# First modulation groups made as columns, and K and Q split earlier, in a diffusion backbone kernel on one core

## Chip, core and metric

The kernel runs as one program on 1 core of a Trainium2 chip. The metric is the device time of one execution in microseconds (us); lower is better. TensorE is written PE below, VectorE DVE, ScalarE ACT, and the queue that issues most of the loads SP.

## What is computed

Two layers of a backbone over 256 latent and 256 context tokens of width 1024, all in f32. Each layer is a gated feed-forward half step, a token mixer (retention with 4 heads beside a short convolution), and a second half step. Every sub-layer starts with a modulated norm. Cut to what the change touches:

```
def adaln_params(cond, w_mod, b_mod):
    m = jax.nn.silu(cond) @ w_mod + b_mod
    return m.reshape(cond.shape[0], 1, N_MOD, D_MODEL)

def modulated_norm(h, w, mod, i):
    return rmsnorm(h, w) * (1.0 + mod[:, :, 3 * i + 1]) + mod[:, :, 3 * i]

def swiglu(y, w_up, w_down):
    a, b = jnp.split(y @ w_up, 2, axis=-1)
    return (jax.nn.silu(a) * b) @ w_down
...
    scores = jnp.einsum('bhnid,bhnjd->bhnij', qf, kf) * intra_decay[None, :, None]
    intra = jnp.einsum('bhnij,bhnje->bhnie', scores, vf)
```

`modulated_norm` of the first sub-layer needs shift and scale (sections 0 and 1 of `w_mod` of layer 0, 2048 columns) before the first product with `w_up` can start. The retention needs K and Q (rotated by the rope), and decay matrices that are sums of masked exponentials.

## The kernel before, in words

Every engine runs an order written out by hand; semaphores join them. A product with a weight is made in single precision out of three fast ones: each weight block of 128x1024 is loaded to `RAW`, ACT copies it to a rounded `HI` (L1066), DVE makes the rest `LO` (L1514), and PE multiplies HI and LO with the high and low half of the activations `Y`. A unit is such a block with its products. There are 6 weight slots, and a load waits until the unit that had the slot before is done.

**The beginning** (stage "ada"). PE turns the rows of x and ctx (L852), ACT and DVE copy them to `H` (`h_copy`). SP loads `w_mod` in 16 blocks `WM` of 512 KB, with the blocks of the first four units between them: WM 0, 1, unit 0, WM 2, 3, unit 1, WM 4, 5, unit 2, WM 6, 7, unit 3, WM 8 to 15. Four blocks make one of four groups `g`; blocks 4g and 4g+1 give its scale (`sec` 1), 4g+2 and 4g+3 its shift (`sec` 0). `modulation(b)` multiplies block b, with the two conditions SiLU(c), SiLU(c_ctx) stationary in 32-column strips `SCW` and 256 columns of the block moving (L812, four strips of the array at once). ACT copies the sums to `ADAROWS` (`rows_out`, L1201), and `columns(g, sec)` turns them to columns on PE (L822). DVE adds the bias (`mods0`, L1737), ACT makes the high half of y (`y0`, L1209), DVE the low half (`y0_full`, `y0_low`, L1753 and L1760). `first_units(ks, units)` is what PE makes of y: for the k-blocks `ks` it adds into the banks of the units (L836, L840). Group g gives y for k = 2g and 2g+1. `keep_clock(n)` are n idle products of ones (L779), which fill stretches of PE. An f32 product that isn't the fast kind is shown by the trace as two records on PE.

**Stage "v"**. PE makes V in 8 steps `cc` (L931). Beside it DVE ropes K and Q in steps 0 to 3; in steps 2 to 5 ACT makes the four exponentials of one head (L1359), which wait for DVE's sums `DEC` of the head before (L1956), and then `KQH`, the rounded copy of two heads of K or Q (L1365). DVE in steps 3 to 6 masks and sums the exponentials (L1953, L1956, L1959) and then makes `KQL`, the rest of K or Q (L1964). Stage "ret" waits on PE for all four `KQL`, then makes the scores (L942 to L944) of heads 0 and 1; DVE multiplies them with `DEC` into `PX` and `PC` (`probs`, L1978), and `outputs(0)` on PE (L970) waits for those.

Of the kernel before, what the change touches and what calls it, by code (L numbers as in the profile page):

```python
# [7 lines left out]
F32 = mybir.dt.float32  # L8
F32R = mybir.dt.float32r
ACT = mybir.ActivationFunctionType  # L10
# [118 lines left out]
def plan():  # L129
# [70 lines left out]
    for at, s in enumerate(p.stages):  # L200
        after = p.stages[at + 1] if at + 1 < len(p.stages) else None
        if s.kind == "ada":
            s.turn = [p.acc(b) for b in (7, 5, 6, 4, 0, 1, 2, 3)]
            s.vec_acc = p.acc(6)
            s.rb_acc = p.acc(6)
            s.rows = [[p.acc(4), p.acc(5)] for g in range(4)]
            s.cols_acc = [[p.acc(6), p.acc(7)] for g in range(4)]
            after.halves = []
        elif s.kind in ("up", "k"):
# [99 lines left out]
def build(nc, x, c, ctx_in, c_ctx, norm_w, w_mod, b_mod, up1, down1, w_in, log_decay, conv_w,  # L309
# [76 lines left out]
    with es:  # L386
# [99 lines left out]
        def drain_wait(eng, acc):  # L486

            eng.wait_ge(drained[acc.bank], acc.use)
# [17 lines left out]
        def follows(s):  # L506
            return stages[stages.index(s) + 1]
# [110 lines left out]
        def _(pe):  # L618
# [180 lines left out]
            for s in stages:  # L799
                T = s.T  # L800
                if s.kind == "ada":
                    up_s = follows(s)

                    def modulation(b):

                        g, sec = b // 4, 1 - b % 4 // 2
                        acc = s.rows[g][sec]
                        if b % 2 == 0:
                            bank_wait(pe, acc)
                        pe.wait_ge(wm_landed[b], 16)  # L810
                        for kk in range(4):
                            ins = mm(B[acc.bank][32 * kk:32 * kk + 32, 0:GROUP], SCW[:, 4 * (b % 2) + kk, :],  # L812
                                     WM[b][:, kk, :], start=(b % 2 == 0), stop=(b % 2 == 1),
                                     tile_position=(0, 32 * kk))
                        ins.then_inc(wm_used, 1)
# [45 lines left out]
                                            ).then_inc(vec_turned, 1)  # L861
                    pe.wait_ge(sc_wide, 1)
                    modulation(0)
                    drain_wait(pe, s.turn[0])
                    keep_clock(3, s.turn[0].bank)
                    modulation(1)
                    bank_wait(pe, s.rb_acc)
                    pe.wait_ge(diag_done, 4)
                    mm(B[6][:], ONES[:], DIAG[:], start=True, stop=True).then_inc(rb0_done, 1)
                    columns(0, 1)  # L870
                    drain_wait(pe, s.turn[6])
                    keep_clock(5, s.turn[6].bank)
                    modulation(2)
                    keep_clock(3, s.turn[6].bank)
                    modulation(3)
                    keep_clock(2, s.turn[6].bank)
                    columns(0, 0)
                    drain_wait(pe, s.turn[7])
                    keep_clock(5, s.turn[7].bank)
                    first_units((0, 1), (0,))  # L880
                    modulation(4)
                    modulation(5)
                    first_units((0, 1), (1,))
                    columns(1, 1)
                    first_units((0, 1), (2,))
                    modulation(6)
                    modulation(7)
                    columns(1, 0)
                    first_units((0, 1), (3,))
                    first_units((2,), range(4))  # L890
                    first_units((3,), (0, 1))
                    for b in range(8, 12):
                        modulation(b)
# [162 lines left out]
        def _(act):  # L1056
# [136 lines left out]
            for s in stages:  # L1193
                T, cols = s.T, s.cols
                if s.kind == "ada":
                    def rows_out(g, sec):
                        acc = s.rows[g][sec]
                        act.wait_ge(wm_used, 4 * g + 4 - 2 * sec)
                        if g >= 2:
                            act.wait_ge(cols_done, 2 * (g - 1) - sec)  # L1200
                        A(ADAROWS[:, g % 2, sec, :], B[acc.bank][:, 0:GROUP], ACT.Copy).then_inc(drained[acc.bank], 1)  # L1201

                    def y0(*ks):
# [13 lines left out]
                    act.wait_ge(x_summed, 3)  # L1217
                    act.wait_ge(ctx_summed, 1)
                    A(RT4[:], SS4[:], ACT.Sqrt, bias=EPST[:, 0:1], scale=1.0 / D).then_inc(x_rooted, 1)
                    h_copy(0, 1, 3)  # L1220
                    rows_out(0, 1)
                    h_copy(6)
                    split_upto(0)
                    rows_out(0, 0)
                    y0(0, 1)
                    split_upto(2)
                    rows_out(1, 1)
                    split_upto(3)
                    rows_out(1, 0)
                    y0(2, 3)  # L1230
                    rows_out(2, 1)
                    rows_out(2, 0)
                    y0(4)
# [110 lines left out]
                elif s.kind == "v":  # L1344
# [3 lines left out]
                    for cc in range(8):  # L1348
                        step(s.u + cc)
                        if cc == 0:  # L1350
                            swapped(s.layer, 1, QTT, stages[stages.index(s) - 1].acc)
                        if 2 <= cc < 6:

                            h = cc - 2
                            f, b = LG[:, lgw + h:lgw + h + 1], LG[:, lgw + HEADS + h:lgw + HEADS + h + 1]
                            for n, (col, g) in enumerate(((CM_RELP, f), (CM_RELN, b), (CM_CF, f), (CM_CB, b))):
                                if h or s.layer:
                                    act.wait_ge(dec_done, 2 * (HEADS * s.layer + h) - (1 if n < 2 else 0))
                                A(G4[:, n, :], CM[:, col:col + 512], ACT.Exp, scale=g).then_inc(exp_done, 1)  # L1359
                        if 2 <= cc < 6:  # L1360

                            g = cc - 2
                            heads, n = slice(2 * (g % 2), 2 * (g % 2) + 2), 512 if g < 2 else follows(s).T
                            act.wait_ge(rope_done, 4 * s.layer + g + 1)
                            A(KQH[:, heads, g // 2, 0:n], (KTT, QTT)[g // 2][:, heads, 0:n], ACT.Copy).then_inc(kq_hi, 1)  # L1365
                        if cc % 4 == 3:
                            act.wait_ge(unit_done, s.u + cc + 1)
                            for tt in range(4):
                                b = s.acc[4 * (cc // 4) + tt].bank
                                A(V[:, tt, (cc // 4) * 512:(cc // 4 + 1) * 512], B[b][:], ACT.Copy  # L1370
                                  ).then_inc(drained[b], 1)
# [132 lines left out]
        def _(dve):  # L1504
# [221 lines left out]
            for s in stages:  # L1726
                T, cols = s.T, s.cols
                if s.kind == "ada":
# [68 lines left out]
                    split_upto(2)  # L1797
                    xn(2, 3)
                    mods0(1, 1)
                    split_upto(3)  # L1800
                    mods0(1, 0)
                    y0_full(2)
                    y0_low(2)
                    y0_full(3)
                    y0_low(3)
                    xn(4, 5, 6, 7)
# [112 lines left out]
                elif s.kind == "v":  # L1919
# [5 lines left out]
                    for cc in range(8):  # L1925
                        step(s.u + cc)
                        if cc < 4:
# [16 lines left out]
                                             ).then_inc(rope_part, 1)  # L1944
                            dve.wait_ge(rope_part, 2 * n + 2)
                            V_.tensor_tensor(src, a, b, ALU.add).then_inc(rope_done, 1)
                        if 3 <= cc < 7:

                            h = cc - 3
                            e, dp = 4 * (HEADS * s.layer + h), 2 * (HEADS * s.layer + h)  # L1950
                            for n, (g, op) in enumerate(((0, ALU.is_ge), (1, ALU.is_le))):
# [6 lines left out]
                            dve.wait_ge(exp_done, e + 4)  # L1958
                            V_.tensor_tensor(DEC[:, h, 2:4, :].rearrange("p a n -> p (a n)"), G4[:, 2, :], G4[:, 3, :],  # L1959
                                             ALU.add).then_inc(dec_done, 1)  # L1960
                            g = cc - 3
                            heads, n = slice(2 * (g % 2), 2 * (g % 2) + 2), 512 if g < 2 else follows(s).T
                            dve.wait_ge(kq_hi, 4 * s.layer + g + 1)
                            V_.tensor_tensor(KQL[g // 2][:, heads, 0:n], (KTT, QTT)[g // 2][:, heads, 0:n],  # L1964
                                             KQH[:, heads, g // 2, 0:n].bitcast(F32), ALU.subtract).then_inc(kq_lo, 1)
                elif s.kind == "ret":
                    nP, nO = s.nP, s.nO
                    dve.wait_ge(dec_done, 2 * HEADS * (s.layer + 1))
# [190 lines left out]
```

## Time and profile before

| | |
|---|---|
| median of 3 runs | 2143.64 us (2143.31 to 2145.12) |
| profiled execution, its own time | 2144.41 us |
| its span, first to last instruction | 2142.5 us |
| PE busy | 2128.9 us, 99% |
| DVE busy | 1410.8 us, 66% |
| ACT busy | 785.3 us, 37% |
| mean granted clock of PE | 0.999 |
| mean rate of loads | 148 GB/s |

The span is what instructions cover; the 1.9 us beyond it lie around it. Busy time of PE counts records that overlap in its pipeline, so that the start-to-start distance of records tells what one costs, not its length.

### The profile page before, as it was taken

The numbers are of one execution on the slowest core, as the hardware profiler recorded it, in microseconds if no ns is written. First come the engines' busy times: TensorE is split into PE (matmuls) and PEld (weight loads), VectorE is DVE, ScalarE is ACT, GpSimd is POOL, SyncE is SP. The second block draws the span as 40 slices with busy tenths as digits, with TensorE's granted clock in tenths as the row PEclk, the third lists the DMA queues.
The fourth block names the chain that finished last, engine by engine and source line by source line (L and its number), as shares of the span: only waits on it lengthen the run. The fifth ranks groups of instructions, "written<-read, shape, count | busy, mean of one in ns | idle before, by whom it ended". The sixth has DMA issues, their size and how long they took to land.

```text
span 2142.5 us, 26254 instructions
## 1 busy us (share of the span) xinstructions
PE 2128.9 (99%) x10667; PEld 1803.6 (84%) x10667; DVE 1410.8 (66%) x1929; ACT 785.3 (37%) x1158; POOL 0.2 (0%) x4
## 2 busy tenths in 40 slices
PE   9999999999999999999999999999999999999998
PEld 6888888988888888898888888888889888888887
DVE  5677777657588873477777767733335678777765
ACT  4322222444322222342222234222223555556654
POOL 0000000000000000000000000000000000000000
PEclk9999999999999999999999999999999999999999
DMA  8655555341455553345555544433333537775664
GB/s 261 196 168 176 158 166 163 123 117 38 123 164 157 177 157 94 94 139 166 175 165 163 163 141 141 135 98 99 91 99 106 157 90 200 205 213 139 187 189 145
DMA packets 454395, 318.13 MB, mean 148 GB/s; under 512 B 10478, under 2 KB 429702, under 8 KB 453894
## 3 DMA queue, kind: packets, MB, share of 16 engines
q1 hardware_dynamic: 432476, 243.43, 39.4%
q10 hardware_dynamic: 21800, 73.03, 10.0%
q8 instruction: 85, 1.39, 0.3%
q14 instruction: 34, 0.28, 0.0%
HBM read 312.23 MB, written 1.05 MB: 146 GB/s over the span
## 4 chain that ended last, share of the span: by engine, by line
PE 96%; DVE 1%; ACT 1%; SPq 1%; DMA 0%; issue 0%; DVEq 0%
PE bank L628 23%; PE bank L630 23%; PE bank L629 23%; PE bank L626 9%; PE bank L627 5%; PE bank L659 2%; PE bank L931 2%; PE bank L970 1%; PE bank L693 1%; PE bank L694 1%; PE bank L695 1%; PE bank L663 1%; SPq L551 1%; PE bank L836 1%; PE bank L769 0%; ACT G L1359 0%
## 5 line engine op out<-in xcount | busy, mean ns | idle before, releaser
L1514 DVE TENSOR_TENSOR LO<-RAW,HI 128x1024 fp32r<-128x1024 f32 (+1 forms) x435 | 522.9, 1206 | 344.9 <-ACT HI L1066 344.7
L628 PE MATMUL bank<-Y,HI 128*128 128x512 f32 (+1 forms) x1440 | 555.7, 386 | 0.0
L630 PE MATMUL bank<-Y,LO 128*128 128x512 f32 (+1 forms) x1440 | 553.6, 384 | 0.0
L629 PE MATMUL bank<-Y,HI 128*128 128x512 f32 (+1 forms) x1440 | 553.5, 384 | 0.0
L1066 ACT ACTIVATE HI<-RAW 128x1024 fp32r<-128x1024 f32 (+1 forms) x435 | 441.6, 1039 | 118.0 <-DVE MODACC L1525 36.3
L628 PEld LDWEIGHTS bank<-Y,HI 128*128 128x128 f32 x1440 | 270.6, 188 | 54.2 <-issue 1.3
L630 PEld LDWEIGHTS bank<-Y,LO 128*128 128x128 f32 x1440 | 270.6, 188 | 54.0
L629 PEld LDWEIGHTS bank<-Y,HI 128*128 128x128 f32 x1440 | 270.7, 188 | 53.4 <-issue 0.5
L1525 DVE SCALAR_TENSOR_TENSOR MODACC<-MODRAW,SC,MODACC 128x1024 f32<-128x1024 f32 x224 | 277.2, 1279 | 3.7 <-DMA MODRAW<-in_w_mod_dram 3.3
L626 PE MATMUL bank<-Y,HI 128*128 128x512 f32 x720 | 253.8, 397 | 0.0
L628 PE MATMUL bank<-Z,HI 128*128 128x512 f32 (+1 forms) x594 | 218.0, 367 | 0.0
L630 PE MATMUL bank<-Z,LO 128*128 128x512 f32 (+1 forms) x594 | 217.1, 366 | 0.0
L629 PE MATMUL bank<-Z,HI 128*128 128x512 f32 (+1 forms) x594 | 217.1, 365 | 0.0
L1257 ACT ACTIVATE TMP<-bank 128x512 f32<-128x512 f32 x66 | 39.5, 598 | 455.9 <-PE bank L630 372.2
L627 PE MATMUL bank<-Y,LO 128*128 128x256 f32 x720 | 201.1, 279 | 0.0
L626 PEld LDWEIGHTS bank<-Y,HI 128*128 128x128 f32 x720 | 135.2, 188 | 32.3
L627 PEld LDWEIGHTS bank<-Y,LO 128*128 128x128 f32 x720 | 135.7, 188 | 0.1
L628 PEld LDWEIGHTS bank<-Z,HI 128*128 128x128 f32 x594 | 112.0, 189 | 18.2
L629 PEld LDWEIGHTS bank<-Z,HI 128*128 128x128 f32 x594 | 112.1, 189 | 18.1
L630 PEld LDWEIGHTS bank<-Z,LO 128*128 128x128 f32 x594 | 112.0, 189 | 17.8
L1634 DVE SCALAR_TENSOR_TENSOR H<-bank,GATE,H 128x256 f32<-128x256 f32 x64 | 28.3, 479 | 122.1 <-PE bank L630 122.1
L1836 DVE TENSOR_TENSOR TMP<-bank,TMP 128x512 f32<-128x512 f32 x66 | 45.5, 690 | 74.7 <-PE bank L630 74.7
(276 smaller groups left out, 2422.8 us busy)
## 6 DMA issues: line engine op xcount, KB each, us to landing
RAW<-in_ffn_w_up_dram SPq DMA_DIRECT2D x174, 512.0 KB, 3.9
MODRAW<-in_w_mod_dram ACTq DMA_DIRECT2D x128, 512.0 KB, 4.4
RAW<-in_w_in_dram SPq DMA_DIRECT2D x128, 512.0 KB, 4.1
RAW<-in_ffn_w_down_dram SPq DMA_DIRECT2D x66, 512.0 KB, 4.0
RAW<-in_ffn_w_down_dram SPq DMA_DIRECT2D x24, 384.0 KB, 3.5
WM<-in_w_mod_dram SPq DMA_DIRECT2D x16, 512.0 KB, 8.9
RAW<-in_w_ret_out_dram SPq DMA_DIRECT2D x16, 512.0 KB, 4.8
RAW<-in_w_conv_out_dram SPq DMA_DIRECT2D x16, 512.0 KB, 4.5
```

Of the source, the lines that this page charges most:

```text
L626: mm(bank[:].rearrange("p (a n) -> p a n", a=2), hi, X[:, k, :, cols], start=first, stop=False)
L627: return mm(bank[:, 0:HALF], lo, X[:, k, 0, cols], start=False, stop=end)
L628: mm(bank, hi, X[:, k, 0, cols], start=first, stop=False)
L629: mm(bank, hi, X[:, k, 1, cols], start=False, stop=False)
L630: return mm(bank, lo, X[:, k, 0, cols], start=False, stop=end)
L659: mm(B[cc][:, cols], wblock(s.u + cc, part, k), Y[:, k, 0, cols], start=(k == 0 and part == 0), stop=False)
L931: ins = mm(B[s.acc[4 * half + tt].bank][:], Y[:, k, a, tt * P:(tt + 1) * P], w[u % SLOTS][:, kk * 512:(kk + 1) * 512], start=(k == 0 and ( ...
L1066: A(weights(v, 0), raw_weights(v), ACT.Copy).then_inc(hi_done, 1)
L1257: A(TMP[:, o % 2, cols], B[s.acc[cc].bank][:, cols], ACT.Silu).then_inc(drained[s.acc[cc].bank], 1)
L1514: V_.tensor_tensor(weights(v, 1), raw_weights(v), weights(v, 0).bitcast(F32), ALU.subtract).then_inc(lo_done, 1)
L1525: V_.scalar_tensor_tensor(acc, MODRAW[i % 2][:], a, acc, ALU.mult, ALU.add).then_inc(mod_step, 1)
L1836: V_.tensor_tensor(TMP[:, 2 + o % 2, cols], B[s.acc[cc].bank][:, cols], TMP[:, o % 2, cols], ALU.mult).then_inc(drained[s.acc[cc].bank], 1)
```

## The change

Groups 0 and 1 of the modulation (blocks 0 to 7) are multiplied the other way round: the block is stationary, 128 columns at a time, and the two conditions move, so that the sums come out as columns. `rows_out` and `columns` of these groups go. The order of PE's beginning is rewritten, with other counts for `keep_clock`; the fourth unit (unit 3) joins at k = 2 instead of before it, and `HI` and `LO` of unit 3 come later on ACT and DVE. In stage "v" `KQH` is made one step earlier and ahead of the exponentials, and `KQL` one step earlier and ahead of the masks.

```
             s.rb_acc = p.acc(6)
-            s.rows = [[p.acc(4), p.acc(5)] for g in range(4)]
+            s.rows = [[p.acc(4), p.acc(5)] if g >= 2 else None for g in range(4)]
...
                         g, sec = b // 4, 1 - b % 4 // 2
+                        if g < 2:
+                            acc = s.cols_acc[g][sec]
+                            if b % 2 == 0:
+                                bank_wait(pe, acc)
+                            pe.wait_ge(wm_landed[b], 16)
+                            for kk in range(4):
+                                for m in range(2):
+                                    ins = mm(B[acc.bank][:, 2 * m:2 * m + 2], WM[b][:, kk, m * P:(m + 1) * P],
+                                             SC[:, :, 4 * (b % 2) + kk], start=(b % 2 == 0 and kk + m == 0),
+                                             stop=(b % 2 == 1 and kk == 3 and m == 1))
+                            if b % 2 == 1:
+                                ins.then_inc(cols_done, 1)
+                            return
...
                     modulation(0)
-                    drain_wait(pe, s.turn[0])
-                    keep_clock(3, s.turn[0].bank)
-                    modulation(1)
                     bank_wait(pe, s.rb_acc)
                     pe.wait_ge(diag_done, 4)
                     mm(B[6][:], ONES[:], DIAG[:], start=True, stop=True).then_inc(rb0_done, 1)
-                    columns(0, 1)
+                    modulation(1)
+                    drain_wait(pe, s.turn[1])
+                    keep_clock(8, s.turn[1].bank)
+                    modulation(2)
+                    keep_clock(5, s.turn[1].bank)
+                    modulation(3)
                     drain_wait(pe, s.turn[6])
-                    keep_clock(5, s.turn[6].bank)
-                    modulation(2)
-                    keep_clock(3, s.turn[6].bank)
-                    modulation(3)
-                    keep_clock(2, s.turn[6].bank)
-                    columns(0, 0)
                     drain_wait(pe, s.turn[7])
-                    keep_clock(5, s.turn[7].bank)
+                    keep_clock(7, s.turn[1].bank)
                     first_units((0, 1), (0,))
                     modulation(4)
                     modulation(5)
                     first_units((0, 1), (1,))
-                    columns(1, 1)
                     first_units((0, 1), (2,))
                     modulation(6)
                     modulation(7)
-                    columns(1, 0)
-                    first_units((0, 1), (3,))
-                    first_units((2,), range(4))
+                    keep_clock(6, s.turn[7].bank)
+                    first_units((2,), range(3))
+                    first_units((0, 1, 2), (3,))
                     first_units((3,), (0, 1))
...
-                    h_copy(0, 1, 3)
-                    rows_out(0, 1)
-                    h_copy(6)
+                    h_copy(0, 1, 3, 6)
                     split_upto(0)
-                    rows_out(0, 0)
                     y0(0, 1)
                     split_upto(2)
-                    rows_out(1, 1)
+                    y0(2)
                     split_upto(3)
-                    rows_out(1, 0)
-                    y0(2, 3)
+                    y0(3)
...
                     mods0(1, 1)
-                    split_upto(3)
                     mods0(1, 0)
                     y0_full(2)
                     y0_low(2)
+                    split_upto(3)
```

PE, the beginning, from the first modulation to the first unit. Before (`SCW` the conditions, `WM_72` to `WM_75` blocks 0 to 3, `x4` instructions in a row):

```order
L812 MATMUL bank<-WM_72,SCW 32x256 x4
L779 MATMUL bank<-ONES 128x128 x3
L812 MATMUL bank<-WM_73,SCW 32x256 x4
L869 MATMUL bank<-DIAG,ONES 128x512
L822 MATMUL bank<-CK,ADAROWS 128x2 x2
L779 MATMUL bank<-ONES 128x128 x5
L812 MATMUL bank<-WM_74,SCW 32x256 x4
L779 MATMUL bank<-ONES 128x128 x3
L812 MATMUL bank<-WM_75,SCW 32x256 x4
L779 MATMUL bank<-ONES 128x128 x2
L822 MATMUL bank<-CK,ADAROWS 128x2 x2
L779 MATMUL bank<-ONES 128x128 x5
```

And of the changed kernel, the same place on PE:

```order
L814 MATMUL bank<-SC,WM_72 128x2 x8
L879 MATMUL bank<-DIAG,ONES 128x512
L814 MATMUL bank<-SC,WM_73 128x2 x8
L779 MATMUL bank<-ONES 128x128 x8
L814 MATMUL bank<-SC,WM_74 128x2 x8
L779 MATMUL bank<-ONES 128x128 x5
L814 MATMUL bank<-SC,WM_75 128x2 x8
L779 MATMUL bank<-ONES 128x128 x7
```

A modulation is now 8 instructions of the form that `columns` had (128 stationary columns, 2 moving) in place of 4, and 20 idle products stand where 18 did, with the two `columns` gone.

PE further on, where unit 3 (`HI_112`, `LO_106`) joins. Before, from blocks 6 and 7:

```order
L812 MATMUL bank<-WM_78,SCW 32x256 x4
L812 MATMUL bank<-WM_79,SCW 32x256 x4
L822 MATMUL bank<-CK,ADAROWS 128x2 x2
L836 MATMUL bank<-Y,HI_112 128x512
L836 MATMUL bank<-Y,LO_106 128x512
L840 MATMUL bank<-Y,HI_112 128x512
```

And of the changed kernel:

```order
L814 MATMUL bank<-SC,WM_78 128x2 x8
L814 MATMUL bank<-SC,WM_79 128x2 x8
L779 MATMUL bank<-ONES 128x128 x6
L849 MATMUL bank<-Y,HI_109 128x512
L849 MATMUL bank<-Y,LO_103 128x512
L849 MATMUL bank<-Y,HI_110 128x512
```

Units 0 to 2 take k = 2 first, and unit 3 stands behind them with its nine products.

DVE in stage "v" of layer 0, the last head (`G` the exponentials, `LO` the split of a later unit). Before:

```order
L1514 TENSOR_TENSOR LO_104<-RAW_98,HI_110 128x1024
L1953 SCALAR_TENSOR_TENSOR G_55<-CM,G_55 128x512 x2
L1956 TENSOR_TENSOR DEC<-G_55 128x512
L1959 TENSOR_TENSOR DEC<-G_55 128x512
L1964 TENSOR_TENSOR KQL_66<-QTT,KQH 128x1024
L1514 TENSOR_TENSOR LO_105<-RAW_99,HI_111 128x1024
L1978 TENSOR_TENSOR PX<-bank,DEC 128x512 x2
```

And of the changed kernel, one step more:

```order
L1516 TENSOR_TENSOR LO_103<-RAW_97,HI_109 128x1024
L1954 TENSOR_TENSOR KQL_66<-QTT,KQH 128x1024
L1962 SCALAR_TENSOR_TENSOR G_55<-CM,G_55 128x512 x2
L1965 TENSOR_TENSOR DEC<-G_55 128x512
L1968 TENSOR_TENSOR DEC<-G_55 128x512
L1516 TENSOR_TENSOR LO_104<-RAW_98,HI_110 128x1024
L1962 SCALAR_TENSOR_TENSOR G_55<-CM,G_55 128x512 x2
L1965 TENSOR_TENSOR DEC<-G_55 128x512
L1968 TENSOR_TENSOR DEC<-G_55 128x512
L1516 TENSOR_TENSOR LO_105<-RAW_99,HI_111 128x1024
L1982 TENSOR_TENSOR PX<-bank,DEC 128x512 x2
```

The last `KQL` has moved ahead of the masks of head 2 and stands between a split and those masks.

## Rows read from the trace of the kernel before

**Rows 1.** PE's waits, whole span: for what, us in total, times, longest us

```profile
PE bank L942 <- DVE KQL L1964: 1.9, 2, 1.6
PE bank L822 <- ACT ADAROWS L1201: 1.4, 2, 1.2
```

**Rows 2.** Timeline of PE, beginning: start us, us, form, records [idle before]

```profile
15.69 1.12 PE L869 MATMUL bank<-DIAG,ONES 128*128 128x512 f32 x2
...
17.01 1.36 PE L779 MATMUL bank<-ONES 128*128 128x128 f32 x10
18.30 0.64 PE L812 MATMUL bank<-WM,SCW 128*32 128x256 f32 x8
...
25.58 1.07 PE L812 MATMUL bank<-WM,SCW 128*32 128x256 f32 x16
26.58 0.50 PE L836 MATMUL bank<-Y,HI 128*128 128x512 f32 x1
...
34.13 0.47 PE L836 MATMUL bank<-Y,HI 128*128 128x512 f32 x1 [0.36 <-issue]
...
38.31 0.39 PE L836 MATMUL bank<-Y,HI 128*128 128x512 f32 x1
```

**Rows 3.** Timeline of PE's weight loads, beginning

```profile
20.94 0.52 PEld L822 LDWEIGHTS bank<-CK,ADAROWS 128*128 128x128 f32 x4
21.38 1.20 PEld L779 LDWEIGHTS bank<-ONES 128*128 128x128 f32 x10
```

**Rows 4.** Timeline of ACT and DVE, beginning

```profile
12.52 1.55 ACT L1215 ACTIVATE H<-bank 128x512 f32<-128x512 f32 x3
21.59 0.16 DVE L1737 TENSOR_TENSOR MODS<-bank,VT 128x4 f32<-128x4 f32 x1
...
31.72 1.06 ACT L1066 ACTIVATE HI<-RAW 128x1024 fp32r<-128x1024 f32 x1 [3.40 <-DMA RAW<-in_ffn_w_up_dram]
32.80 1.23 DVE L1514 TENSOR_TENSOR LO<-RAW,HI 128x1024 fp32r<-128x1024 f32 x1 [2.03 <-ACT HI L1066]
34.19 2.08 ACT L1209 ACTIVATE Y<-XN,MODS,AMUL 128x256 fp32r<-128x256 f32 x4 [1.14 <-issue]
```

**Rows 5.** Stage "v" of layer 0: ACT and DVE

```profile
459.85 2.56 ACT L1359 ACTIVATE G<-CM,LG 128x512 f32<-128x512 f32 x4 [5.15 <-DVE DEC L1956]
...
479.17 2.56 ACT L1359 ACTIVATE G<-CM,LG 128x512 f32<-128x512 f32 x4 [3.22 <-DVE DEC L1956]
481.63 1.04 ACT L1365 ACTIVATE KQH<-QTT 128x1024 fp32r<-128x1024 f32 x1
482.58 2.00 ACT L1066 ACTIVATE HI<-RAW 128x1024 fp32r<-128x1024 f32 x2
...
487.33 1.22 DVE L1964 TENSOR_TENSOR KQL<-QTT,KQH 128x1024 fp32r<-128x1024 f32 x1
488.47 1.22 DVE L1514 TENSOR_TENSOR LO<-RAW,HI 128x1024 fp32r<-128x1024 f32 x1
489.69 1.34 DVE L1978 TENSOR_TENSOR PX<-bank,DEC 128x512 f32<-128x512 f32 x2
491.05 0.69 DVE L1978 TENSOR_TENSOR PC<-bank,DEC 128x512 f32<-128x512 f32 x1
```

**Rows 6.** End of stage "v" and scores on PE, layer 0, then layer 1

```profile
486.58 0.39 PE L931 MATMUL bank<-HI,Y 128*128 128x512 f32 x1
488.61 0.38 PE L942 MATMUL bank<-KQH 128*128 128x256 f32 x1 [1.64 <-DVE KQL L1964]
493.01 3.62 PE L970 MATMUL bank<-PX,V 128*128 128x256 f32 x16
1721.12 0.39 PE L931 MATMUL bank<-HI,Y 128*128 128x512 f32 x1
1721.75 0.39 PE L942 MATMUL bank<-KQH 128*128 128x256 f32 x1 [0.24 <-DVE KQL L1964]
```

**Rows 7.** PE, PEld, DVE, ACT, POOL busy, granted clock, DMA share, GB/s

```profile
24.00:38.00 14.00, 11.45 (x73) 7.67 (x73) 9.40 (x18) 5.60 (x9) 0.00 (x0) 1.00 1.08 337
```

More of the change, by code:

```diff
@@ L1197, in rows_out @@
                         acc = s.rows[g][sec]
-                        act.wait_ge(wm_used, 4 * g + 4 - 2 * sec)
-                        if g >= 2:
-                            act.wait_ge(cols_done, 2 * (g - 1) - sec)
+                        act.wait_ge(wm_used, 4 * g - 4 - 2 * sec)
                         A(ADAROWS[:, g % 2, sec, :], B[acc.bank][:, 0:GROUP], ACT.Copy).then_inc(drained[acc.bank], 1)
@@ L1351, in _ @@
                             swapped(s.layer, 1, QTT, stages[stages.index(s) - 1].acc)
+                        if 1 <= cc < 5:
+                            g = cc - 1
+                            heads, n = slice(2 * (g % 2), 2 * (g % 2) + 2), 512 if g < 2 else follows(s).T
+                            act.wait_ge(rope_done, 4 * s.layer + g + 1)
+                            A(KQH[:, heads, g // 2, 0:n], (KTT, QTT)[g // 2][:, heads, 0:n], ACT.Copy).then_inc(kq_hi, 1)
                         if 2 <= cc < 6:
@@ L1359, in _ @@
                                 A(G4[:, n, :], CM[:, col:col + 512], ACT.Exp, scale=g).then_inc(exp_done, 1)
[L1360 to L1365, printed above, removed]
                         if cc % 4 == 3:
@@ L1946, in _ @@
                             V_.tensor_tensor(src, a, b, ALU.add).then_inc(rope_done, 1)
+                        if 2 <= cc < 6:
+                            g = cc - 2
+                            heads, n = slice(2 * (g % 2), 2 * (g % 2) + 2), 512 if g < 2 else follows(s).T
+                            dve.wait_ge(kq_hi, 4 * s.layer + g + 1)
+                            V_.tensor_tensor(KQL[g // 2][:, heads, 0:n], (KTT, QTT)[g // 2][:, heads, 0:n],
+                                             KQH[:, heads, g // 2, 0:n].bitcast(F32), ALU.subtract).then_inc(kq_lo, 1)
                         if 3 <= cc < 7:
@@ L1960, in _ @@
                                              ALU.add).then_inc(dec_done, 1)
[L1961 to L1965, printed above, removed]
                 elif s.kind == "ret":
```

## The prediction

> **What bounds the kernel now.** I read the page first: PE is busy for 99% of the span, and the chain that ended last lies on PE for 96% of it. So a change counts only by what it does to PE's queue: instructions put in or taken out, and waits. The waits of PE come next. The longest is that of the scores for `KQL`, 1.9 us in two places, the second that of `columns` for `ADAROWS`, 1.4 us [rows 1]. Those are the two places that the change touches, and together they are 3.3 us of 2142.5, about 0.15%. That is the first thing to see: even if both waits went and cost nothing, the gain would be less than the 0.2% that a measurement of this kernel can tell from no change (4.3 us; "same" below means within it).
>
> In the beginning I then read the timeline of PE, of its weight loads, and of ACT and DVE. Two chains meet there. One is PE's own queue. The other is the load of unit 3, of which HI starts at 31.72 and LO ends at 34.03 [rows 4]; PE starts on unit 3 at 34.13, when LO is there [rows 2]. From there to 38.31 it makes 18 fast products, 0.232 us each [rows 2], and from 38.31 on its order is the same in both kernels. The start of that product (k = 3 of unit 0) is my milestone: what it moves by is what the beginning gives or takes.
>
> **The price of a modulation.** Before, blocks 4 and 5 took PE from 25.58 to 26.58, so one block costs 0.50 us [rows 2]. The new form has no row of its own, but `columns` is the same form: 128 stationary f32 columns, 2 moving. An instruction is two records, and four records of it take the weight path from 20.94 to 21.38, 0.11 us each [rows 3]. The idle products, with 64 times as many moving columns, need 0.11 us too (ten loads in 1.20 us, of which the last is about 0.19) [rows 3]. So the load of the weights sets the price, and the two moving columns don't make it cheaper. A block has 8 instructions, 16 records, 1.76 us, and with a small gap to the next group 1.8 us. Eight blocks: 14.4 us in place of 4.0. Against that four `columns` go, 0.44 us each, 1.8 us, and their waits.
>
> The bounds: below, a record can cost what one of the old form does, 1.00 us over 16 records, 0.0625 us [rows 2], a block then 1.0 us. Above, a load could take its whole row length, 0.52 minus three distances of 0.11, 0.19 us [rows 3], a block then 3.0 us. I take 0.11 since it is the same instruction form, with other stationary weights in each.
>
> The Trainium skill, page "TensorE: Matmul & The Clock Gate", section "Back-to-back issue gap", puts a matmul of 1 to 64 columns at about 25 ns (or 62 ns), by which a block would cost 0.4 us to 1.0 us and the beginning would lose nothing. The same page's section "LDWEIGHTS" gives columns / 1.2 ns, 107 ns for 128 columns; with that rule the trace agrees (0.11 us).
>
> **The beginning, walked through.** PE can start modulation(0) when the first `h_copy` is done. The three take 1.55 us from 12.52, the first ends at about 13.1 [rows 4]; with a latency, 13.2.
> - modulation(0) to 15.0, the norm's product to 15.9 (it starts at 15.69 before and is modelled with 1.12; I take 0.9 to the next) [rows 2], modulation(1) to 17.7.
> - keep_clock(8): keep_clock(5) takes 17.01 to 18.30, 1.29 us [rows 2]; three more are six records, 0.66; 1.95 us, to 19.65. modulation(2) to 21.45, keep_clock(5) to 22.75, modulation(3) to 24.6.
> - DVE's `mods0` of the shift then starts at 24.75. It was 21.59 [rows 4]. From it to the end of unit 0's k = 0, 1 before was 25.58 - 21.59 = 3.99 us [rows 2, 4], and nothing in that piece changes: 28.7.
> - modulation(4), (5) to 32.3, units 1 and 2 (12 products of 0.232) to 35.1, modulation(6), (7) to 38.8. Their weights' HI and LO are made during this.
> - `mods0` at 39.0, ACT's y of k = 2 from 39.2 to 40.3 (half of the 2.08 us that four pieces take) [rows 4]. keep_clock(6) lasts to 40.35 and is just covered. Nine products of units 0 to 2 to 42.5. HI of unit 3 stands behind y(2) on ACT: 40.2 to 41.3 (1.06), LO behind `y0_low(2)` on DVE, to 42.55 (1.23) [rows 4]. Unit 3 takes its nine products to 44.7.
>
> The milestone goes from 38.31 [rows 2] to 44.7: **+6.4 us**. The load of unit 3, which set it before, landed 8 us ahead of its use and is no limit any more; the gain for which unit 3 joins later (2 us of products ahead of its LO) has nothing left to hide, since LO itself is now late behind ACT's y(2). Loads of `WM` 8 to 15 and of units 4 and 5 don't wait for PE, so nothing queues behind on SP; the seventh unit's load waits for unit 0 and moves with PE.
>
> **Stage "v" and the scores.** In layer 0 the last product of V starts at 486.58 and would be followed by the next at about 486.81; the scores start at 488.61 [rows 6]. In the changed kernel the last `KQL` stands one head earlier, near 479, so the scores start at once, and their 36 records (4.40 us to 493.01 [rows 6]) end at 491.2. What is late next is DVE, for `outputs(0)` needs `probs(0)`. I walk its chain. Ahead of the first exponentials ACT now has two `KQH`, and the second waits for the rope of K; ahead of the first masks DVE has two `KQL`. This puts the second head's exponentials from 459.85 to about 463.5. V's copies (2 us) and a split follow there, of which part was waiting time, so the third head is 1.85 us late and the fourth starts at 481.2 in place of 479.17 [rows 5]. Behind it `KQH` (0.95) and `KQL` (1.14) are gone from the path [rows 5]. So `probs(0)` starts at 489.65, as good as unchanged from 489.69, and its three pieces end at 491.7 [rows 5]. `outputs(0)` starts at 491.85 in place of 493.01: **-1.15 us** of the 1.8 us. The bounds: nothing if DVE is over 1.1 us later than I make it, 1.8 if it is 0.6 earlier. In layer 1 PE has 0.4 us between 1721.35 and 1721.75 [rows 6]. By the same walk `probs(0)` starts 0.8 us later than before, but PE makes a unit of the next stage between scores and outputs, which covers it: **-0.4 us**.
>
> **The sum.** +6.4 - 1.15 - 0.4 = +4.85 us. On the profiled execution (2144.41 = 2142.5 of span and 1.9 around it) that is 2149.3; it ran 0.8 us above the median, so on the median it is 2143.64 + 4.85 = 2148.5, 0.23% slower.
>
> **The rivals.**
> - *The 2-column products are cheap* (not slower). In the changed kernel 16 of them stand in a row, and weights could load behind them faster than in the short groups of before. At 0.0625 us a record, modulation(3) ends at 21.3, about where `columns` ended, and unit 3's load is the limit again. Its LO is put behind y(2), which costs what the later joining saves; the milestone lands within 0.3 of 38.31. Total 0.3 - 1.55 = -1.25: 2142.4. For it speaks that the idle products would then fill exactly the time up to the landing of the next block; against it the 0.11 us of the same form. Each 0.01 us off a record's price takes 1.3 us off the loss (128 records), so the sign turns near 0.07 us. 0.17. The Trainium skill's 25 ns rule (page and section "Back-to-back issue gap" as above) would lead to this case.
> - *The clock falls.* Granted is 1.00 in all stages of the beginning [rows 7], but 3.6 us of 2-column products in a row, twice, have no counterpart there. If PE falls from 2.4 to 1.2 GHz behind modulation(7), the 18 products behind it take 4.2 us more: 2152.7. The idle products ahead and behind speak against it. 0.08. The Trainium skill, the page named above, section "Part 1: The HAM clock gate (the "warmup" mystery)", says that an idle PE is gated down; no row here shows whether such products count as idle.
> - *Stage "v" gives nothing*, because the exponentials' chain is over 1 us later than I have it: 2143.64 + 6.4 = 2150.0. 0.08.
> - *The forecast*, 2146.5 to 2151: 0.62. What is left, 0.05, is a middle price of a record.
>
> **How the numbers follow.** The forecast's own spread (gaps between groups, a price of 0.10 or 0.12 us, 128 records each) is 1.3 us either way around +4.85, so some 0.38 of its 0.62 is over 4.3 us and 0.24 within. Slower: 0.38 + 0.08 + 0.08 = 0.54. Same: 0.24, 0.15 of the cheap case and 0.03 of the rest: 0.42. Faster: 0.04, since even the cheap case stays within 0.2%. The range goes from 2144.5, the middle price of a record, to 2152.7, the clock case; outside are the cheap case and a little more, 0.2.
>
> **What would show it.** A block of the first two groups takes PE 1.7 to 1.9 us; the first `mods0` of a shift at 24 to 25.5; unit 0 at k = 3 near 44.7; granted clock 1.00; no wait of the scores for `KQL`, and `outputs(0)` about 0.6 us after the scores' end in layer 0 by a wait for `probs`. Wrong would be I, above all, with a modulation of well under 1.5 us.

## The result, and the profile after

| | before | after |
|---|---|---|
| median of 4 runs each, in turn | 2144.36 us | 2160.34 us (2156.75 to 2162.75) |
| ratio | 1 | 1.0075 [1.0063, 1.0087] |
| profiled execution: time, span | 2144.41, 2142.5 us | 2158.04, 2156.1 us |
| mean granted clock of PE | 0.999 | 0.994 |
| PE busy | 2128.9 us, 99% | 2147.2 us, 100% |

The change costs 16 us, 0.75%. I had said 4.9 us. The range, 2144.5 to 2152.7, doesn't hold the result.

The timeline of PE in the beginning, the counterpart of [rows 2] (columns as there):

```profile
13.07 1.92 PE L814 MATMUL bank<-SC,WM 128*128 128x2 f32 x16 [0.53 <-ACT H L1221]
14.85 1.10 PE L879 MATMUL bank<-DIAG,ONES 128*128 128x512 f32 x2
15.79 3.16 PE L814 MATMUL bank<-SC,WM 128*128 128x2 f32 x16
18.82 3.76 PE L779 MATMUL bank<-ONES 128*128 128x128 f32 x16
22.37 2.09 PE L814 MATMUL bank<-SC,WM 128*128 128x2 f32 x16
24.32 1.36 PE L779 MATMUL bank<-ONES 128*128 128x128 f32 x10
25.52 2.70 PE L814 MATMUL bank<-SC,WM 128*128 128x2 f32 x16
28.08 3.33 PE L779 MATMUL bank<-ONES 128*128 128x128 f32 x14
31.07 0.77 PE L849 MATMUL bank<-Y,HI 128*128 128x512 f32 x1
...
40.09 0.63 PE L849 MATMUL bank<-Y,HI 128*128 128x512 f32 x1
40.51 0.63 PE L849 MATMUL bank<-Y,LO 128*128 128x512 f32 x1
...
48.79 0.77 PE L849 MATMUL bank<-Y,HI 128*128 128x512 f32 x1
...
53.65 0.39 PE L849 MATMUL bank<-Y,HI 128*128 128x512 f32 x1
```

Read the distances between starts of groups that follow each other. The first block takes 14.85 - 13.07 = 1.78 us. The second, the same 16 records, takes 18.82 - 15.79 = 3.03 us. The idle products that follow make it plainer: 16 records of ones need 22.37 - 18.82 = 3.55 us in one place, 10 of them 25.52 - 24.32 = 1.20 us in the next: 0.22 and 0.12 us a record. A fast product takes 0.42 us at 40.09 and 0.23 us before. Different work that grows by about a factor of two together, and for a while only, is the clock. The milestone (k = 3 of unit 0, 38.31 in [rows 2]) starts at 53.65: +15.3 us.

The same stretches by windows, the counterpart of [rows 7]: PE, PEld, DVE, ACT, POOL busy, then the granted clock, DMA share and GB/s:

```profile
10.00:16.00 6.00, 5.47 (x45) 4.79 (x43) 3.86 (x11) 4.40 (x10) 0.00 (x0) 1.00 1.03 317
16.00:20.00 4.00, 4.00 (x20) 4.00 (x20) 2.95 (x7) 1.06 (x1) 0.00 (x0) 0.51 1.13 328
20.00:25.00 5.00, 5.00 (x35) 5.00 (x34) 1.68 (x2) 0.00 (x0) 0.00 (x0) 0.71 1.13 327
25.00:30.00 5.00, 5.00 (x32) 5.00 (x31) 1.27 (x4) 1.49 (x4) 0.00 (x0) 0.63 1.10 325
30.00:35.00 5.00, 5.00 (x28) 4.53 (x27) 4.89 (x8) 2.47 (x4) 0.00 (x0) 0.69 1.10 347
35.00:40.00 5.00, 5.00 (x25) 4.51 (x26) 0.56 (x3) 0.00 (x0) 0.00 (x0) 0.65 1.10 351
40.00:45.00 5.00, 5.00 (x26) 4.33 (x24) 0.00 (x0) 0.00 (x0) 0.00 (x0) 0.66 1.07 285
45.00:50.00 5.00, 5.00 (x30) 4.81 (x30) 2.62 (x5) 3.02 (x5) 0.00 (x0) 0.68 0.03 9
50.00:55.00 5.00, 5.00 (x22) 3.87 (x21) 3.95 (x8) 0.00 (x0) 0.00 (x0) 0.98 0.00 0
```

The clock is 0.51 from 16 to 20, so PE is at 1.2 GHz there, and between 0.63 and 0.71 up to 50: it changes between 1.2 and 2.4 GHz. PE is busy for 100% of each of these windows from 16 on. In windows of 0.25 us it falls near 16.1, 26.3, 36.5 and 46.8: three times within two-column products (modulation(1), (3) and (5)), the fourth time just behind modulation(7), in the idle products. It rises near 23, 33, 43 and 50. Two of the rises, 23 and 43, fall into modulation(2) and (6): such a product doesn't hold the clock down either. Length times (1 - clock), summed over the windows from 16 to 55, is 12.0 us of work lost.

Stage "v" and the scores, PE, layers 0 and 1, the counterpart of [rows 6]:

```profile
501.91 0.39 PE L939 MATMUL bank<-HI,Y 128*128 128x512 f32 x1
502.14 0.28 PE L950 MATMUL bank<-KQH 128*128 128x256 f32 x1
507.07 2.18 PE L978 MATMUL bank<-PX,V 128*128 128x256 f32 x9 [0.46 <-DVE PC L1982]
...
1735.26 0.39 PE L939 MATMUL bank<-HI,Y 128*128 128x512 f32 x1
1735.48 0.28 PE L950 MATMUL bank<-KQH 128*128 128x256 f32 x1
```

The scores start at once behind V in both layers. From V's last product to `outputs(0)` it is 5.16 us against 6.43 of before, -1.27; in layer 1 the wait for `KQL` is gone, 0.22 against 0.63, -0.41. DVE, the counterpart of the last two of [rows 5]:

```profile
504.94 1.28 DVE L1982 TENSOR_TENSOR PX<-bank,DEC 128x512 f32<-128x512 f32 x2
506.14 0.68 DVE L1982 TENSOR_TENSOR PC<-bank,DEC 128x512 f32<-128x512 f32 x1
```

The third piece ends at 506.8 and PE starts on `outputs(0)` at 507.07: DVE is the new limit, as walked. +15.34 - 1.27 - 0.41 = +13.66, and the span grew by 13.6. The loss lies in the beginning, whole.

### The profile page after: what moved, and what is told of

Same layout as the page of the kernel before. It is cut to its first block, busy times and chain, and to the rows that moved or that the text cites. A ratio compares the mean times of both kernels' runs of the same rounds, so it can differ in the third digit from the quotient of the medians.

```text
span 2156.1 us, 26371 instructions
## 1 busy us (share of the span) xinstructions
PE 2147.2 (100%) x10731; PEld 1826.5 (85%) x10731; DVE 1410.3 (65%) x1929; ACT 784.5 (36%) x1154; POOL 0.2 (0%) x4
## 4 chain that ended last, share of the span: by engine, by line
PE 97%; DVE 2%; ACT 1%; issue 0%; DVEq 0%; ACTq 0%
PE bank L628 22%; PE bank L630 22%; PE bank L629 22%; PE bank L626 9%; PE bank L627 5%; PE bank L659 2%; PE bank L939 2%; PE bank L978 1%; PE bank L693 1%; PE bank L694 1%; PE bank L695 1%; PE bank L663 1%; PE bank L849 1%; PE bank L814 1%; PE bank L779 1%; PE bank L769 0%
```

## Experiments

Ratios are to the kernel before, run on the same chip in between. The milestone is given from the profile of each.

**Each half alone.** The kernel before with the new order of stage "v" (the first edit below, on ACT; the same move of `KQL` on DVE), and the changed kernel with the old order there.

```
+                        if 1 <= cc < 5:
+                            g = cc - 1
...
+                            A(KQH[:, heads, g // 2, 0:n], (KTT, QTT)[g // 2][:, heads, 0:n], ACT.Copy).then_inc(kq_hi, 1)
                         if 2 <= cc < 6:
...
-                        if 2 <= cc < 6:
-                            g = cc - 2
...
-                            A(KQH[:, heads, g // 2, 0:n], (KTT, QTT)[g // 2][:, heads, 0:n], ACT.Copy).then_inc(kq_hi, 1)
```

> The kernel before with only the earlier split of K and Q (stage v). My step: the scores no longer wait for KQL, outputs(0) of layer 0 starts about 1.2 us after where PE could, waiting for probs; 1.3 to 1.8 us less than before, ratio 0.9992 to 0.9994, clock 0.999. Rival (the part gives nothing, or something else in it costs): within 0.3 us of before or slower.

> The changed kernel with the old order in stage v, so the new beginning alone. If the beginning is the whole loss: k = 3 of unit 0 starts near 53.6 us as in the changed kernel (38.3 before), the granted clock is low in four stretches between 16 and 50 us, and the time is 15 to 18 us above before, 1.5 us above the changed kernel. If part of the loss is in stage v: less than 14 us above before.

Stage "v" alone: 2143.25 us, 0.9993 [0.9984, 1.0002], 0.9 us under before where I had expected 1.3 to 1.8; it is timed again below. The beginning alone: 2160.56 us (2158.84 to 2163.99), 1.0079 [1.0066, 1.0093]; its profiled execution has the milestone at 57.87, +19.6, a span longer by 19.6 us, and the old wait of 1.9 us for `KQL`. So the loss is the beginning's. The 1.7 us of stage "v" don't show between this kernel and the changed one (2160.56 and 2160.34), since executions of either differ by 5 to 6 us. They do so in the beginning: two profiled executions with the same order there have the milestone at 53.65 and 57.87, and this one was at 0.50 of the clock from 16 to 35, in place of the four stretches that I had expected.

**How many columns move.** The changed kernel, with 128 moving columns in each product of the modulation (the two conditions and 126 columns of ones) instead of 2, and with 32 (the conditions and zeros of `SCW`). Order, count of products and idle products stay. What differs is the width, the place in the bank, and for 128 columns the tile `SCX` that DVE fills beforehand.

```
-                                    ins = mm(B[acc.bank][:, 2 * m:2 * m + 2], WM[b][:, kk, m * P:(m + 1) * P],
-                                             SC[:, :, 4 * (b % 2) + kk], ...
+                                    ins = mm(B[acc.bank][:, 128 * m:128 * m + 128], WM[b][:, kk, m * P:(m + 1) * P],
+                                             SCX[:, 4 * (b % 2) + kk, :], ...
```

> The changed kernel with 128 moving columns (2 conditions, 126 columns of ones) in place of 2 in the first two groups' modulation; each product should still take two records of 0.11 us at full clock, and the sums used are the same. Theory: products with 2 moving columns keep the array so idle that the clock falls to its lower level, so with 128 columns the granted clock is 1.00 throughout and k = 3 of unit 0 starts near 44 to 45, total 4 to 6 us above before. Rival (it is not the moving columns but the order, the gaps or the many weight loads): clock falls as before and the total stays 13 to 17 us above before.

> As the run with 128 columns, but 32 moving columns (the strip that the rows form has). Theory: somewhere between 2 and 128; if what counts is the share of time in which columns move, 32 of 128 is still low and the clock falls in at least some of the four stretches, 8 to 16 us above before. Rival (any real strip is enough, or only the count of instructions matters): equal to the run with 128 columns, or equal to the changed kernel to 1 us.

With 128: 2148.54 us (2148.05 to 2148.88), 1.0021 [1.0012, 1.0030]. Windows, and the timeline of PE:

```profile
16.00:20.00 4.00, 4.00 (x38) 4.00 (x37) 3.93 (x8) 0.97 (x1) 0.00 (x0) 1.00 1.13 328
20.00:25.00 5.00, 5.00 (x47) 5.00 (x47) 1.19 (x4) 0.83 (x2) 0.00 (x0) 1.00 1.12 323
```

```profile
12.74 2.02 PE L815 MATMUL bank<-SCX,WM 128*128 128x128 f32 x16 [0.53 <-ACT H L1222]
14.60 1.02 PE L880 MATMUL bank<-DIAG,ONES 128*128 128x512 f32 x2
15.46 1.95 PE L815 MATMUL bank<-SCX,WM 128*128 128x128 f32 x16
17.25 1.95 PE L780 MATMUL bank<-ONES 128*128 128x128 f32 x16
19.03 1.95 PE L815 MATMUL bank<-SCX,WM 128*128 128x128 f32 x16
...
43.73 0.39 PE L850 MATMUL bank<-Y,HI 128*128 128x512 f32 x1
```

64 times as many moving columns cost nothing where the clock is high (1.86 us a block here with its gap, 1.78 there), and the clock is 1.00 in every window up to 55. The milestone is at 43.73: the form of the modulation, with the idle products that go with it, costs 5.4 us, and the 9.9 us from there to 53.65 are the clock's. In the medians of all executions it is 11.8 us, 2160.34 against 2148.54. (Of the 12.0 us of work lost in the changed kernel not all arrive there; the 128-column kernel has waits in between, 0.46 us for `Y` the longest, which slow work covers.) This is the test that decides: the same instructions in the same order, PE busy without a gap from 16 to 25 us in both, only wider. What it doesn't take apart is width and content: the added columns are ones here and zeros in the kernel with 32.

With 32: 2150.25 us (2147.97 to 2156.49), 1.0038 [1.0024, 1.0052]. One fall in the profiled execution, behind modulation(5):

```profile
25.00:30.00 5.00, 4.54 (x32) 3.59 (x31) 4.56 (x8) 3.73 (x6) 0.00 (x0) 1.00 1.07 316
30.00:35.00 5.00, 5.00 (x26) 4.42 (x26) 1.82 (x5) 0.00 (x0) 0.00 (x0) 0.66 1.07 344
35.00:40.00 5.00, 5.00 (x40) 4.74 (x39) 0.00 (x0) 0.00 (x0) 0.00 (x0) 1.00 1.10 349
```

Its milestone is at 45.83, of which 0.67 is the first block's later start (13.41 for 12.74), for its load. 32 lies between 2 and 128 in the number of falls and in the milestone. Its executions lie 8.5 us apart, against 0.8 for 128 columns and 6.0 for 2, and their mean granted clocks say why: 0.995 in the three near 2156.3, 0.998 or 0.999 in the four others.

**Do the idle products help?** The changed kernel without its 26; the changed kernel with an edit that was to spread 32 of them, one behind every first of two modulation products, in place of the groups (this one also waits for the bank of the idle products first); and the 128-column kernel without its 26.

```
                             for kk in range(4):
                                 for m in range(2):
...
                                              stop=(b % 2 == 1 and kk == 3 and m == 1))
+                                if m == 0:
+                                    keep_clock(1, s.turn[1].bank)
```

> The changed kernel without its 26 idle products (keep_clock 8, 5, 7, 6). Theory (the blocks of 2-column products let the clock fall, and idle products standing in groups between them don't hold it): the clock falls all the same, with low stretches of the same kind; what the idle products cost, 5.7 us at full clock and more at the low one, comes back, so the total is 6 to 11 us below the changed kernel, still 4 to 10 above before. Rival (the idle products are what holds what clock there is): lower mean clock and the total within 4 us of the changed kernel.

> The changed kernel with its idle products not in groups but one behind every first of two 2-column products, 32 in all (26 before), so that a third of a block's records move 128 columns. Theory (what counts is how much of a stretch columns move): the clock holds much better, two low stretches at most, total 5 to 9 us above before, 7 us or more below the changed kernel. Rival (any block with 2-column products lets it fall, however mixed): 15 us above before as the changed kernel.

> 128 moving columns and no idle products. If the rest of the loss (4.4 us above before with 128 moving columns) is PE's time for the weight loads of the new form plus the idle products on its path: clock 1.00, k = 3 of unit 0 starts 3 to 5 us ahead of the run with idle products (43.7 us), limited then by the landing of the blocks, total within 1.5 us of before. Rival (the idle products fill time that PE waits anyway): within 1.5 us of the run with them.

| | ratio | milestone |
|---|---|---|
| 2 columns, idle products in groups | 1.0075 [1.0063, 1.0087] | 53.65 |
| 2 columns, none | 1.0057 [1.0042, 1.0072] | 53.79 |
| 2 columns, none, one more wait (meant as spread) | 1.0063 [1.0048, 1.0078] | 56.55 |
| 128 columns, in groups | 1.0021 [1.0012, 1.0030] | 43.73 |
| 128 columns, none | 1.0009 [0.9999, 1.0018] | 43.03 |

The edit of the third row doesn't do what it was meant to. Its `if m == 0` stands behind the loop over `m` and not in it. There `m` is always 1, so none of the 32 idle products is made. The trace shows it: 44 records of ones, the last at 8.0 us, as in the kernel without any, and 96 in the changed kernel. The 48 records of modulation(1) to (3) take the same time in both. Without idle products:

```profile
15.57 10.24 PE L814 MATMUL bank<-SC,WM 128*128 128x2 f32 x48
```

And in the kernel of the edit:

```profile
17.85 10.24 PE L814 MATMUL bank<-SC,WM 128*128 128x2 f32 x48
```

So this is a second kernel without idle products, and whether spread ones would hold the clock isn't tested: what was expected of it is neither met nor missed.

The two kernels without idle products are at 0.50 from 16 to 40, where the changed kernel is at 0.51 to 0.71. They are no slower for it: 2156.5 and 2157.7 us, against 2160.3 and 2160.6 for the two kernels with groups, with intervals of the ratios that overlap. I had expected 6 to 11 us less without them, and it is 3.8, within the 4 us of the rival. So the groups don't prevent the falls, and no run shows that they pay for themselves. Whether they shorten the low stretches is open. The first one lasts from 14.8 to 42 us and from 14.7 to 42 without them, from 16.1 to 22.9 and from 14.5 to 35 with them, one profiled execution each; the mean clocks of all executions overlap (0.991 to 0.994 without, 0.991 to 0.995 with).

Without idle products the 128-column kernel has one fall (0.66 in 25 to 30, behind waits of PE for `Y`, 1.5 us at 21.7), and it is faster than with them, by 2.2 us: 2.1 above its before against 4.4 (the intervals just overlap, but the highest of its ten executions, 2147.37 us, is below the lowest of the ten others, 2148.05). Its milestone is 0.7 us earlier, where I had expected 3 to 5. It also repeats the test of width without idle products: milestone 43.03, against 53.79 and 56.55 with 2 columns. In the kernel of the misplaced edit the span grew by 14.2 us, less than its milestone by 4 us. Stage "v" gives 1.7 of that; where the stages behind it gave the rest back I didn't follow.

**What before leaves, and the late unit 3.** In the profiled execution of stage "v" alone the clock fell once in the beginning, in the old form too. PE had waited 1.15 us for `ADAROWS`:

```profile
30.37 1.07 PE L812 MATMUL bank<-WM,SCW 128*32 128x256 f32 x16
32.59 0.58 PE L822 MATMUL bank<-CK,ADAROWS 128*128 128x2 f32 x4 [1.15 <-ACT ADAROWS L1201]
33.53 0.47 PE L836 MATMUL bank<-Y,HI 128*128 128x512 f32 x1 [0.36 <-issue]
...
34.84 0.63 PE L836 MATMUL bank<-Y,LO 128*128 128x512 f32 x1
35.27 0.63 PE L840 MATMUL bank<-Y,HI 128*128 128x512 f32 x1
...
39.34 0.39 PE L836 MATMUL bank<-Y,HI 128*128 128x512 f32 x1
```

So I filled that wait, on top of the new stage "v": five idle products ahead of `columns(1, 0)`. And in another kernel I took only the late joining of unit 3, with the rows form kept.

```
                     modulation(7)
+                    keep_clock(5, s.turn[7].bank)
                     columns(1, 0)
```

```
-                    first_units((0, 1), (3,))
-                    first_units((2,), range(4))
+                    first_units((2,), range(3))
+                    first_units((0, 1, 2), (3,))
```

> The kernel before with the earlier split of K and Q, and five idle products between modulation(7) and the last columns of group 1, where PE waits 1.2 us for ADAROWS. In the profile of the run with the split alone the clock fell to 0.74 between 35 and 40 us, behind this wait. If such a fall explains most of the spread from run to run: clock 1.00 in all of the beginning, total 1.5 to 2.5 us below before and below the run without the fill by 0.3 to 1.5. Rival (the fill only lengthens PE's path): 0.1 to 0.5 above the run without it.

> The kernel before with the earlier split of K and Q, the rows form kept, and only the joining of unit 3 at k = 2 taken from the change (with the order of ACT and DVE that goes with it). My step: this joining hides nothing, because HI and LO of unit 3 are late behind y(2) in turn; k = 3 of unit 0 starts within 0.5 us of 38.3 and the total is that of the run with the split alone, 2142 to 2143.5. Rival (the joining is worth what it says, nine products of 0.23 us ahead of unit 3's LO): up to 2 us less, 2140.5 to 2141.5.

With the fill: 2141.85 us (2141.19 to 2142.45), 0.9991 [0.9982, 1.0000], span 2139.9. Its beginning:

```profile
31.07 1.38 PE L779 MATMUL bank<-ONES 128*128 128x128 f32 x10
32.29 0.51 PE L822 MATMUL bank<-CK,ADAROWS 128*128 128x2 f32 x4
32.66 0.48 PE L836 MATMUL bank<-Y,HI 128*128 128x512 f32 x1
...
37.13 0.39 PE L836 MATMUL bank<-Y,HI 128*128 128x512 f32 x1
```

The fill ends when `ADAROWS` is there, the clock is 1.00 throughout, and the milestone is at 37.13. But unit 3's load also landed earlier in this execution, and the kernel without the fill had been timed apart from it. So I ran both again side by side, and the fill alone on the kernel before.

> The kernel before with the new order of stage v alone, once more, now side by side with the two kernels with the fill. Theory A, that the old beginning loses its clock in some executions behind the wait for ADAROWS (one fall cost 1.6 us in the profile of the first such run): executions lie in two groups about 2 us apart, near 2141.5 and 2143.6, median 2142 to 2143.5, spread over 2 us. Theory B, that the fill does nothing but stand in a wait: the same median as the kernel with the fill to 0.5 us, and the same spread.

> The new order of stage v and five idle products in the wait ahead of columns(1, 0). Theory A: executions in one group, within 1.5 us, median 2141.5 to 2142.2, 0.5 to 1.5 us under the kernel without the fill, granted clock 1.00 from 16 to 50. Theory B: within 0.5 us of the kernel without the fill.

> The kernel before with the five idle products alone, stage v as it was. Theory A: 1.7 us above the kernel with both (what stage v measured), so about 2143.5, and 0.3 to 1 us under the kernel before, with a spread under 2 us where that of before is 4. Theory B: the same as the kernel before to 0.3 us, with the same spread of 4 us.

| | median | ratio | lowest to highest |
|---|---|---|---|
| before, 27 runs | 2143.63 us | 1 | 2142.31 to 2146.34 |
| fill only, 11 runs | 2143.63 us | 0.9998 [0.9989, 1.0007] | 2143.10 to 2144.35 |
| stage "v" only, 11 runs | 2141.85 us | 0.9991 [0.9982, 0.9999] | 2141.07 to 2143.50 |
| both, 11 runs | 2141.73 us | 0.9989 [0.9980, 0.9998] | 2141.45 to 2142.84 |

Stage "v" gives 1.8 us without the fill and 1.9 with it. The fill doesn't move the median, where I had expected 0.3 to 1.5 us. What it takes away is the upper part: 10 of the 27 executions of the kernel before stand at 2144.68 or above, a gap of 0.6 us below them, and none of the 11 with the fill. The profiled execution of stage "v" alone had a fall again (0.83 from 30 to 35 and from 35 to 40, behind a wait of 1.25 us for `ADAROWS`), the two with the fill are at 1.00 there. The mean granted clock of each execution says the same: it is 0.998 in seven of the ten upper ones, and 0.999 or 1.0 in all 17 others. Stage "v" alone lies in two groups as well. In its first timing five of 11 executions are at 2142.22 or below and six at 2143.25 or above; in the second three of 11 are at 2143.16 or above. Both profiled executions, each with a fall, are among the upper ones. That is how the same kernel gave 2143.25 once and 2141.85 the other time. So the fall behind that wait comes in a part of the executions, it costs about the 1.6 to 2 us by which the upper ones stand out, and the fill prevents it. That each upper execution has this fall is argued, since only one execution in each run has a trace, and not all scatter is the beginning's: in every profiled execution the clock is also low in the last 1 to 4 us. The kernel with both has the lowest median, 0.1% under before; from stage "v" alone, 0.12 us above it, it can't be told apart.

With the late unit 3: 2143.19 us, 0.9997 [0.9988, 1.0006], milestone at 39.54, where I had expected 38.3 to within 0.5. Nothing to be had, with one fall in its profile as well (0.85 and 0.81 from 30 to 40), behind a wait for `Y` of 1.43 us that this order puts there.

## Why the prediction was wrong

**The price of a modulation** was right. A block at full clock took 1.78 us (predicted 1.76 to 1.8). The cheap rival is out. The Trainium skill, page "TensorE: Matmul & The Clock Gate", section "Back-to-back issue gap", has about 25 ns for an isolated matmul of 1 to 64 columns; here, f32 with new weights in each, it is 0.11 us a record, and the measurement decides.

**The beginning, walked through** is the step that failed: every duration in it was one at 2.4 GHz, so that the sum had the clock at nothing, where it measured 9.9 us. At that clock the walk holds: the 128-column kernel, with the same order, has the milestone at 43.73 (said 44.7, so +5.4 for +6.4), the first `mods0` of a shift at 23.93 (said 24.75), and a time of 2148.5. That this is the predicted time to 0.1 us is in part luck: against its own before it is +4.4 and not +4.85, and that before stood 0.5 us higher. In the changed kernel the walk leaves the rails at 16.1, in modulation(1): `mods0` is at 28.26, the milestone at 53.65.

**The clock rival** had the right mechanism and the wrong place, size and chance. I let the clock fall only once, behind modulation(7), and priced 18 products (+4.2 us). That fall came, as the fourth. The first came 3 us after the start of the new form, in modulation(1), and 15 of the 24 us at half speed were the modulation and the idle products themselves. The term of 4.2 measured 9.9 us. Blocks 0 and 1 have only the norm's product between them, which I didn't count as a row of such products. I gave it 0.08, on the ground that idle products stood ahead and behind. The runs show that groups of them don't hold the clock. [Rows 7] could not speak for this: they show 24 to 38 us only (the trace has 1.00 in all of 10 to 60), and the clock under a form that was about to be taken out. With the price of a row I took care to find the nearest row of the same form. With the clock I took a row of the old kernel as if it held for the new one.

**Unit 3 and the loads** were right as told: no wait of PE for a load of a unit came in, and the late joining alone gave nothing, to the 0.1% that its interval allows.

**Stage "v"** was right, and within 0.15 us: -1.27 and -0.41 where I had -1.15 and -0.4, through the same limit, `probs(0)` on DVE. Timed alone it is -0.9 us (interval over 1) and -1.8 us (just clear of 1), and -1.9 us between the two kernels with the fill, run side by side. The rival that it gives nothing is out.

What is only argued: why few moving columns count for less. The runs show that the added columns decide (2, 32, 128 moving, in the same order), not by what measure, nor whether what stands in them matters. The Trainium skill, the page named above, section "Part 1: The HAM clock gate (the "warmup" mystery)", tells of a PE that is gated down when idle; in this trace PE was busy for 100% of the windows in which it was at 1.2 GHz, so the busy share that a profile shows is no guide to it.

## What to carry to other kernels

Turning a matmul round so that a handful of columns move saves the way back to columns, but it pays the full load of the weights for each 128 columns and, in long runs, can take the clock of everything around it: here 5.4 us for the form with its idle products and 9.9 us for the clock, to save two waits of 3.3 us in all. When a change puts a new form of product on PE in a run of microseconds, the granted clock of the old trace says nothing about it; price the walk at 1.2 GHz as well, and give that case a real chance. If such a form is wanted, widening the moving operand with dummy columns up to 128 cost nothing and kept the clock here, but for one fall behind waits of PE, while groups of idle products between the blocks didn't. And when an edit is meant to put instructions in, count them in the trace: an `if` one level too far out made a run say something about a kernel that never ran.

## What the runs showed of the hardware

- TensorE fell from 2.4 to 1.2 GHz while it was busy without a gap, in a stretch with f32 products of 128x128 stationary and 2 moving columns: 0.51 in 16 to 20, 0.63 to 0.71 up to 50 us. In the three other profiled executions with 2 columns the first fall came at 14.5 to 14.8 us, within or just behind the first block. With 32 moving columns there was one fall in the profiled execution, with 128 and the same order none.
- At 1.2 GHz records bound by the weight load double too: 16 idle records in 3.55 us, against 1.78 us for the same 16 in the 128-column kernel.
- How often the clock falls differs between executions of one kernel, and the spread shows it: 8.5 us with 32 moving columns (three of seven executions near 2156.3, at a mean clock of 0.995, the others under 2150.3, at 0.998 or 0.999), 6 us with 2 columns, 0.8 us with 128 (3.9 us without the idle products).
- A wait of PE of 1.15 to 1.25 us was followed by a fall in two profiled executions (products 0.43 us apart in place of 0.23) and, at 1.16 us, by none in the kernel before. Five idle products in that wait left the clock at 1.00 in all three profiled executions with them.
